# Attention scores of two branches: from full-height products, one head at a time, to 64-row products for two heads

## The chip, the cores and the metric

One core of a Trainium2 chip (trn2) runs the whole kernel. The metric is the device time of one execution in microseconds (us). Before the change it is 309.70 us, the median of three runs (309.48 to 309.84).

## The reference, cut to what matters

A decoder layer with two causal attention branches over the same input (512 tokens, width 1024), all in float32:

```
h = x @ w_in[l]
(qa, ka, va, ga, iq, ik, iw, c_q, c_kv, k_rope, gb) = _split_cols(h)
qa, ka = _rope(qa), _rope(ka)                  # 8 heads of 64
# branch A: each query attends to the 128 keys that a small indexer picked
att = einsum('bthd,btkhd->bhtk', qb, ks) * 64 ** -0.5 ; softmax ; @ v
# branch B: low-rank queries and keys; 64 plain and 32 rotated columns per head
s = (einsum('bthd,bshd->bhts', qn, k_nope) + einsum('bthr,bsr->bhts', qp, k_pe)) * 96 ** -0.5
# the rotated key k_pe is one for all 8 heads ; causal softmax ; @ v
out = concat([o_a * silu(ga), o_b * silu(gb)]) @ w_out[l]
x = layernorm(ALPHA * x + out)
```

## The kernel before

The products are wanted at nearly float32 accuracy. A number is split into a high part of type fp32r and the rest, a low part of type fp32r; TensorE (PE) takes three products, high by high, high by low and low by high. Where operands are left in plain f32, one product call is recorded as two matmuls.

**Stages.** (1) Seven groups of input projections, 8 chunks of 128 rows of `w_in` each, in three products per chunk and token tile (L1067, the helper `products`). ACT makes the high parts of the weights (L496), POOL the low parts (L403). (2) The latent projections for branch B: A_QPE (rotated query columns, 4 token tiles), A_QN (plain query columns, transposed, one PSUM bank for each pair of heads), later A_KN (plain key columns, the same way) and A_VB (values). (3) Branch A's attention, 32 units (L1216, L1219). (4) Branch B's attention, 32 units (L1225), with the output projection of finished token tiles laid in between (L1348, `out_products`). (5) The rest of the output projection and the layer norm.

**Units.** A unit u is one head of one tile of 128 queries. The tiles go in the order 3, 2, 1, 0, so that a unit's keys number N = 512, 384, 256, 128, eight units of each; `NU_A` = 32 units are branch A, the next 32 are branch B. For a unit, PE makes the scores in bank u % 2 of `ps_s`, DVE adds the mask and takes the row maximum (`mask_unit`, L887), ACT takes the exponential (`exp_unit`, L611), PE transposes it (L1275) two units later, ACT copies it (L631; in branch B, DVE adds the low part, `probs_low`, L927), and PE multiplies by the values four units later (L1291 in branch A, L1306 in branch B). The order on every engine is written out by hand: one loop over u on each, in which PE issues `scores(u)`, `transposes(u-2)`, `outputs(u-4)` and then what is due at this u (`PET_AT`, `O_FIRST`, `A_HALF_AT`). `scores(u)` waits until the mask of unit u-2 is done, `transposes` until a bank of `ps_pT` is free and the exponential is there.

**Branch A's scores.** `qaT` and `kaT` hold for every head the high part in 64 partitions and the low part in the other 64. One product of `qaT` with `kaT` gives high by high plus low by low; one with `kaT_swap`, the same array with its halves exchanged by eight DMAs (L329), gives the cross terms. So a unit costs two full-height fp32r products.

**Branch B's scores.** `qbT` and `kbT` hold 96 partitions for each head, 64 plain and 32 rotated, in plain f32: one product call a unit (L1225), two matmul records. ACT and DVE copy them out of PSUM in halves (L617, L895). The rotated query columns are transposed at u = `PET_AT` = 8 (L1242, 8 transposes), the rotated key at u = 14 (L1249, 4 transposes) and copied to all heads by a DMA (L347). Their values go to SBUF by four copies on ACT (L603), four on DVE (L872) and one on ACT (L685).

**Output weights.** SP loads eight pieces of `w_out` (k = 0 to 7): k < 4 into `w_raw`, the others into `wo_early`. POOL casts them to `wo_hi` (L444) and, for k < 4, makes the low part (L448), in the order `WO_ORDER`. `oT0`, into which ACT writes at u = `O_FIRST` + 2 = 24 (`copy_oT_hi(0, 0)`, L645), lies on `wo_early`, so that ACT waits there until all sixteen `wo_hi` halves are written.

Of the kernel before, what the change touches and what calls it, by code (L numbers as in the profile page):

```python
# [6 lines left out]
P = 128  # L7
# [20 lines left out]
def build(nc, x, xT, positions, freqs, w_in, q_norm_g, w_uq, kv_norm_g, w_ukv, w_out, ln_g, ln_b, out):  # L28
# [81 lines left out]
    qbT = sb("qbT", 0, [B_QK, B_HEADS, SEQ])  # L110
    kaT_swap = sb("kaT_swap", 178, [P, A_HEADS, SEQ], f32r)
# [6 lines left out]
    x_res = sb("x_res", 178, [P, 2, D_MODEL])  # L118
    lng = sb("lng", 186, [P, D_MODEL])
# [15 lines left out]
    kaT = sb("kaT", 98, [P, A_HEADS, SEQ], f32r)  # L135
# [4 lines left out]
    kbT = sb("kbT", 114, [B_QK, B_HEADS, SEQ])  # L140
# [8 lines left out]
    qaT = sb("qaT", 162, [P, A_HEADS, SEQ], f32r)  # L149
# [33 lines left out]
    iw, half_pi = col(TT * IDX_HEADS), col(1)  # L183
# [7 lines left out]
    with ExitStack() as ctx:  # L191
# [13 lines left out]
        kaT_swapped, kpe_copied, stored = sem("kaT_swapped"), sem("kpe_copied"), sem("stored")  # L205
# [51 lines left out]
        A_QPET, A_KPET = A_END + 2, A_END + 6  # L257
# [7 lines left out]
        ACC_LAST = [last_seen([*range(A_END), A_QPET, A_QPET + 1, A_KPET], b) for b in range(4)]  # L265
# [41 lines left out]
        def _(sp):  # L307
# [17 lines left out]
            for n in range(F_KT, F_END):  # L325
                sp.wait_ge(side_read[n % 4], seen(n) + 2)
                h = 2 * (n - F_KT)
                for a in range(2):
                    sp.dma_start(kaT_swap[A_DIM * a:A_DIM * (a + 1), h:h + 2, :].bitcast(f32),  # L329
                                 kaT[A_DIM * (1 - a):A_DIM * (2 - a), h:h + 2, :].bitcast(f32)).then_inc(kaT_swapped, 16)  # L330
# [6 lines left out]
            for k in range(1, KT // 2):  # L337
                load(C_OUT // 2 + k)
# [3 lines left out]
            sp.wait_ge(acc_ready, A_END + 2)  # L342
            load(C_OUT // 2)
            for k in (6, 7):
                load_early(k)
            sp.wait_ge(acc_read[2], ACC_LAST[2])
            sp.dma_start(kbT[NOPE:B_QK, 1:B_HEADS, :],  # L347
                         kbT[NOPE:B_QK, 0:1, :].broadcast_to([ROPE_D, B_HEADS - 1, SEQ])).then_inc(kpe_copied, 16)
            sp.wait_ge(scores_ready, NU_A)
            for k in range(KT // 2, KT):  # L350
                sp.dma_start(wo_raw_b[:, k - KT // 2], w_out_v[:, k]).then_inc(raw_b_loaded[k - KT // 2], 16)
            sp.dma_start(lng[:, :], ln_g.broadcast_to([P, D_MODEL])).then_inc(ln_loaded, 16)
# [15 lines left out]
        def _(pool):  # L368
# [10 lines left out]
                               base=0, pattern=[[-1, P]], channel_multiplier=1).then_inc(const_ready, 1)  # L379
            def rotate_queries(m):  # L380
# [30 lines left out]
            for m in range(TT):  # L411
# [13 lines left out]
                pool.tensor_tensor(src[:, :, 0], t1[:, :, 0], t2[:, :, 0], ALU.subtract).then_inc(qpe_rotated, 1)  # L425
                pool.tensor_tensor(src[:, :, 1], t1[:, :, 1], t2[:, :, 1], ALU.add).then_inc(qpe_rotated, 1)
# [55 lines left out]
        def _(act):  # L482
# [58 lines left out]
            def high_parts(first, i):  # L541

                dst, n = (qaT if first == F_QT else kaT), first + i
                act.wait_ge(side_ready, n + 1)
                for a in range(2):
                    rows = slice(A_DIM * a, A_DIM * (a + 1))
                    act.activation(dst[rows, 2 * i + a, :], side[rows, n % 4], ACT.Copy).then_inc(a_hi_ready, 1)
# [51 lines left out]
            def evac_qpeT(j):  # L599

                quad, r = divmod(j, 2)
                act.wait_ge(acc_ready, A_END + quad + 1)
                ins = act.activation(qbT[NOPE:B_QK, 4 * quad + r, :], ps_y[32 * r:32 * r + 32, quad], ACT.Copy)  # L603
                if r == 1:
                    ins.then_inc(acc_read[2 + quad], 1)

# [59 lines left out]
            for u in range(NU + T_LAG):  # L666
# [14 lines left out]
                if 0 <= u - PET_AT - 1 < 4:  # L681
                    evac_qpeT(u - PET_AT - 1)
                if u == PET_AT + 7:
                    act.wait_ge(acc_ready, A_END + 3)
                    act.activation(kbT[NOPE:B_QK, 0, :], ps_y[0:ROPE_D, 0], ACT.Copy).then_inc(acc_read[2], 2)  # L685
# [14 lines left out]
        def _(dve):  # L700
# [112 lines left out]
            dve.sem_inc(kpe_rotated, 1)  # L813
# [45 lines left out]
            for first, dst in ((F_QT, qaT), (F_KT, kaT)):  # L859
                for h in range(A_HEADS):  # L860
                    n, a = first + h // 2, h % 2
                    rows, low = slice(A_DIM * a, A_DIM * (a + 1)), slice(A_DIM * (1 - a), A_DIM * (2 - a))
                    dve.wait_ge(a_hi_ready, 2 * (n - F_QT) + a + 1)
                    ins = V.tensor_tensor(dst[low, h, :], side[rows, n % 4], dst[rows, h, :], ALU.subtract)
                    if a == 1:
                        ins.then_inc(side_read[n % 4], 2)

            def evac_qpeT(j):
# [131 lines left out]
            for u in range(NU):  # L1000
                if u >= 2:
                    mask_unit(u)
# [389 lines left out]
PET_AT = 8  # L1392
# [45 lines left out]
```

## Time and profile before

| | |
|---|---|
| median of 3 runs | 309.70 us |
| the profiled execution itself | 309.57 us |
| its span, first to last instruction | 307.7 us |
| mean granted TensorE clock | 0.995 |
| PE busy (matmuls) | 294.7 us, 96% of the span |
| PEld busy (weight loads) | 253.4 us, 82% |
| DVE, ACT, POOL busy | 235.3, 170.9, 158.7 us |
| stage 3, branch A's attention | about 177 to 214.5 us |
| stage 4, branch B's attention | about 214.5 to 278 us |

Busy time of an engine is the time in which at least one of its instructions runs. Matmuls overlap: the next one starts while the last one is still running out, so what a matmul costs in a dense stream is the distance from its start to the next start, not its own duration. The chain of waits gives that distance: it follows the work that ended last backwards and charges each piece only with the time until the next. A row of a table of stretches gives, after its length, the busy time of PE, PEld, DVE, ACT and POOL in that order. A row of a timeline begins with its start, then its length, the engine, the line, the operation, `out<-in`, the shape and how many instructions were merged; in brackets stands how long the engine sat idle before it and who released it.

### The profile page before, as it was taken

To read this page: it belongs to the slowest core of one execution; us is meant where nothing else is said; L and a number is where in the kernel's file an instruction comes from. 1 tells how busy PE (TensorE), PEld (TensorE's weight loads), DVE (VectorE), ACT (ScalarE), POOL (GpSimd) and SP (SyncE) were. 2 spreads that over 40 slices of the span, in tenths; PEclk is the share of its full clock that TensorE was granted. 3 is DMA by queue.
4 is the path that set the end of the run, shared out by engine and by line. 5 is a ranking of instruction groups with operands and counts; after the bars stand their busy time and mean duration, and the time that the engine had idled before them with its cause. 6 is when DMAs were issued, how large, how long until landed. Compare 5 with 4: busy or idle time off the path is not lost.

```text
span 307.7 us, 5163 instructions
## 1 busy us (share of the span) xinstructions
PE 294.7 (96%) x1646; PEld 253.4 (82%) x1646; DVE 235.3 (76%) x540; ACT 170.9 (56%) x411; POOL 158.7 (52%) x180
## 2 busy tenths in 40 slices
PE   7979999999999999999999999999999999999990
PEld 7969988888888888888889789998677777888890
DVE  1959967888999999996043644855789998987785
ACT  5843274575242262374357787998867885554200
POOL 4869855303999975535326697820492010335211
PEclk9999999999999999999999999999999999999998
DMA  7947442200434532320058333230950000040411
GB/s 253 342 129 207 136 139 71 68 2 0 117 91 136 154 112 78 102 68 2 0 136 205 140 137 117 90 62 8 350 192 0 2 0 3 0 137 2 136 68 68
DMA packets 14777, 31.24 MB, mean 102 GB/s; under 512 B 1728, under 2 KB 4288, under 8 KB 14752
## 3 DMA queue, kind: packets, MB, share of 16 engines
q1 hardware_dynamic: 14192, 30.60, 32.6%
q10 hardware_dynamic: 560, 0.33, 0.4%
q8 instruction: 13, 0.21, 0.3%
q14 instruction: 12, 0.10, 0.1%
HBM read 26.28 MB, written 2.10 MB: 92 GB/s over the span
## 4 chain that ended last, share of the span: by engine, by line
PE 87%; DVE 5%; issue 2%; DMA 2%; ACT 2%; SPq 0%; POOL 0%; DVEq 0%; ACTq 0%; POOLq 0%
PE ps L1067 46%; PE ps L1348 14%; PE ps L1275 6%; PE ps L1225 5%; PE ps L1291 5%; PE ps L1306 3%; PE ps L1216 2%; DMA w_raw<-in_w_in 2%; PE ps L1219 2%; PE ps L1132 1%; DVE x_lo L717 1%; PE ps L1151 1%; PE ps L1320 1%; PE ps L1122 1%; ACT oT L645 1%
## 5 line engine op out<-in xcount | busy, mean ns | idle before, releaser
L403 POOL TENSOR_TENSOR w_lo<-w_raw,w_hi 128x512 fp32r<-128x512 f32 (+3 forms) x62 | 79.3, 1298 | 41.1 <-ACT w_hi L496 41.0
L1067 PE MATMUL ps<-w_hi,x_hi 128*128 128x512 f32 (+2 forms) x220 | 83.2, 378 | 2.9 <-POOL w_lo L403 1.5
L1067 PE MATMUL ps<-w_hi,x_lo 128*128 128x512 f32 (+2 forms) x220 | 82.0, 373 | 0.0
L1067 PE MATMUL ps<-w_lo,x_hi 128*128 128x512 f32 (+2 forms) x220 | 82.0, 373 | 0.0
L496 ACT ACTIVATE w_hi<-w_raw 128x512 fp32r<-128x512 f32 (+3 forms) x62 | 36.2, 591 | 73.3 <-PE ps L1067 72.3
L1067 PEld LDWEIGHTS ps<-w_hi,x_hi 128*128 128x128 f32 x220 | 41.4, 188 | 9.8 <-issue 2.7
L1067 PEld LDWEIGHTS ps<-w_hi,x_lo 128*128 128x128 f32 x220 | 41.3, 188 | 6.5
L1067 PEld LDWEIGHTS ps<-w_lo,x_hi 128*128 128x128 f32 x220 | 41.4, 188 | 5.9
L1348 PE MATMUL ps<-wo_hi,oT 128*128 128x512 f32 (+1 forms) x144 | 44.3, 372 | 0.0
L611 ACT ACTIVATE probs<-probs,small 128x512 f32<-128x512 f32 (+3 forms) x64 | 35.7, 558 | 11.0 <-DVE small L887 10.5
L1275 PE MATMUL ps<-ident,probs 128*128 128x128 f32 x160 | 28.3, 274 | 1.9 <-ACT probs L611 0.9
L1275 PEld LDWEIGHTS ps<-ident,probs 128*128 128x128 f32 x160 | 20.1, 140 | 11.3 <-issue 6.3
L1348 PEld LDWEIGHTS ps<-wo_hi,oT 128*128 128x128 f32 x144 | 25.7, 189 | 3.3
L840 DVE MATCH_REPLACE8 score<-small,score 128x256 f32<-128x256 f32 (+2 forms) x48 | 25.6, 542 | 0.0
L887 DVE CUSTOM_DVE_ANT_0 probs<-ps,score 128x512 f32<-128x512 f32 (+2 forms) x24 | 13.3, 556 | 14.4 <-PE ps L1219 14.4
L837 DVE MAX8 small<-score 128x8 f32<-128x256 f32 (+2 forms) x48 | 23.5, 545 | 0.0
L1225 PE MATMUL ps<-kbT,qbT 96*128 96x512 f32 (+3 forms) x64 | 22.7, 435 | 0.0
L1291 PE MATMUL ps<-va,probsT 128*128 128x64 f32 x160 | 21.4, 264 | 0.0
L1291 PEld LDWEIGHTS ps<-va,probsT 128*128 128x128 f32 x160 | 20.6, 193 | 0.6 <-issue 0.6
L295 POOL TENSOR_TENSOR obT<-half_sum,crossed 64x128 f32<-64x128 f32 x16 | 8.3, 516 | 24.7 <-DVE oT L919 13.7
L887 DVE CUSTOM_DVE_ANT_0 probs<-ps,causal 128x128 f32<-128x128 f32 (+3 forms) x40 | 17.6, 444 | 3.6 <-PE ps L1225 1.6
L631 ACT ACTIVATE probsT_b<-ps 128x512 fp32r<-128x512 f32 (+3 forms) x32 | 13.8, 431 | 8.4 <-PE ps L1275 8.2
(170 smaller groups left out, 557.4 us busy)
## 6 DMA issues: line engine op xcount, KB each, us to landing
w_raw<-in_w_in SPq DMA_DIRECT2D x20, 512.0 KB, 3.6
kaT_swap<-kaT SPq DMA_DIRECT2D x8, 256.0 KB, 3.7
w_raw<-in_w_out SPq DMA_DIRECT2D x4, 512.0 KB, 5.8
wo_early<-in_w_out SPq DMA_DIRECT2D x4, 512.0 KB, 4.2
wo_raw_b<-in_w_out SPq DMA_DIRECT2D x4, 512.0 KB, 5.1
x_res<-in_x SPq DMA_DIRECT2D x4, 512.0 KB, 7.1
w_raw<-in_w_in SPq DMA_DIRECT2D x4, 416.0 KB, 3.7
x_raw<-in_xT SPq DMA_DIRECT2D x3, 512.0 KB, 6.4
```

The costliest lines, as they stand in the source:

```text
L403: pool.tensor_tensor(w_lo[:, s, 0:n], w_raw[:, s, 0:n], w_hi[:, s, 0:n], ALU.subtract).then_inc(w_lo_ready, 1)
L496: act.activation(dst, w_raw[:, s, 0:n], ACT.Copy).then_inc(w_hi_ready, 1)
L611: act.activation(probs[:, u % NPROBS, 0:N], probs[:, u % NPROBS, 0:N], ACT.Exp, bias=neg_max[:, u % 8:u % 8 + 1], scale=-1.0, accum_out=ro ...
L631: act.activation(dst, ps_pT[:, slot_of[u] % 2, 0:N], ACT.Copy).then_inc(probsT_copied, 1)
L837: step(V.max(top8[:, 8 * j:8 * j + 8], sc))
L840: step(V.match_replace(out=sc, in_to_replace=top8[:, 8 * j:8 * j + 8], in_values=sc, imm_value=TAKEN))
L887: V.tensor_tensor_reduce(out=probs[:, u % NPROBS, 0:N], in0=ps_s[:, u % 2, 0:N], in1=bias, scale=-scale, scalar=3.0e38, op0=ALU.add, op1=A ...
L1067: ins = mm(dst, a, b, start=start and j == 0, stop=stop and j == len(pairs) - 1)
L1225: ins = mm(ps_s[:, b, 0:N], qbT[:, h, t], kbT[:, h, 0:N], start=True, stop=True)
L1275: ins = nc.tensor.transpose(bank[:, j * P:(j + 1) * P], probs[:, u % NPROBS, j * P:(j + 1) * P], ident[:, :])
L1291: ins = mm(ps_o[:, v % 2, h * A_DIM:(h + 1) * A_DIM], probsT[:, u % 3, j * P:(j + 1) * P], va[:, j, h * A_DIM:(h + 1) * A_DIM], start=(j = ...
L1348: ins = mm(out_ps(i, b), oT[i % 2][:, o, k, :], w[:, wcols], start=(r == 0), stop=(r == 3 * KT - 1))
```

## The change

Both branches compute the scores of the two heads of a pair together. The two heads of a pair lie in the two halves of the partitions: head 2p in partitions 0 to 63, head 2p+1 in 64 to 127. High and low parts are separate arrays (`qa_hi`, `qa_lo`, `ka_hi`, `ka_lo`, `qn_hi`, `qn_lo`, `kn_hi`, `kn_lo`). For each term, PE issues one product over 64 rows for the first head and one for the second, into the two banks of `ps_s`. Branch A has three terms, so six products a pair in place of four; branch B has three for the plain columns and two for the rotated ones, so ten fp32r products a pair in place of two f32 product calls (four matmul records).

The rotated query of a head is stored twice in 64 rows (`qr`): its high part in 32 rows and its low part in the next 32; the rotated key's high part (`kr_hi`) and low part (`kr_lo`) are repeated in all four groups of 32 rows. The duplicates are made before the transposes: POOL writes `qpe_dup`, DVE writes `kpe_dup`; then five banks of four transposes each, one bank at each entry of `ROPE_AT`, ACT's high copy and DVE's scalar_tensor_tensor or subtract for each.

Scores, masks and the wait between them go in pairs: PE issues both units of a pair at even u after all earlier masks, DVE masks both at even u. The DMAs that exchanged halves and copied the rotated key are gone. `qpe_dup` lies on a part of `w_raw`, so the loads of the output weights k = 0, 2, 3 move behind the fourth bank of rotated transposes and `WO_ORDER` changes. The loads of the layer norm's constants and of x move behind the last product of branch A with its values.

```
-            for k in range(1, KT // 2):
-                load(C_OUT // 2 + k)
+            load(C_OUT // 2 + 1)
             sp.wait_ge(acc_ready, A_END)
             for k in (4, 5):
                 load_early(k)
-            sp.wait_ge(acc_ready, A_END + 2)
-            load(C_OUT // 2)
             for k in (6, 7):
                 load_early(k)
-            sp.wait_ge(acc_read[2], ACC_LAST[2])
-            sp.dma_start(kbT[NOPE:B_QK, 1:B_HEADS, :],
-                         kbT[NOPE:B_QK, 0:1, :].broadcast_to([ROPE_D, B_HEADS - 1, SEQ])).then_inc(kpe_copied, 16)
+            sp.wait_ge(acc_ready, A_END + 4)
+            for k in (0, 2, 3):
+                load(C_OUT // 2 + k)
...
-                for a in range(2):
-                    rows = slice(A_DIM * a, A_DIM * (a + 1))
-                    act.activation(dst[rows, 2 * i + a, :], side[rows, n % 4], ACT.Copy).then_inc(a_hi_ready, 1)
+                act.activation(dst[:, i, :], side[:, n % 4], ACT.Copy).then_inc(a_hi_ready, 1)
...
+            def rope_high(i):
+
+                act.wait_ge(acc_ready, A_END + i + 1)
+                dst = qr[:, i, :] if i < B_HEADS // 2 else kr_hi[:, :]
+                act.activation(dst, ps_y[:, i % 2], ACT.Copy).then_inc(b_hi_ready, 1)
...
-            for first, dst in ((A_QN, qbT), (A_KN, kbT)):
+            for first, dst in ((A_QN, qn_hi), (A_KN, kn_hi)):
                 for p in range(4):
                     act.wait_ge(acc_ready, first + p + 1)
-                    act.activation(dst[0:NOPE, 2 * p, :], acc[0:NOPE, p], ACT.Copy).then_inc(acc_read[p], 1)
+                    act.activation(dst[:, p, :], acc[:, p], ACT.Copy).then_inc(b_hi_ready, 1)
...
+            def rope_low(i):
+
+                dve.wait_ge(b_hi_ready, 8 + i + 1)
+                if i < B_HEADS // 2:
+                    dve.wait_ge(low_rows_ready, 4)
+                    ins = V.scalar_tensor_tensor(out=qr[:, i, :], in0=qr[:, i, :], scalar=low_rows, in1=ps_y[:, i % 2],
+                                                 op0=ALU.mult, op1=ALU.add)
+                else:
+                    ins = V.tensor_tensor(kr_lo[:, :], ps_y[:, i % 2], kr_hi[:, :], ALU.subtract)
+                ins.then_inc(acc_read[2 + i % 2], 2)
...
-            for first, dst in ((A_QN, qbT), (A_KN, kbT)):
+            for first, hi, lo in ((A_QN, qn_hi, qn_lo), (A_KN, kn_hi, kn_lo)):
                 for p in range(4):
-                    dve.wait_ge(acc_ready, first + p + 1)
-                    V.tensor_copy(dst[0:NOPE, 2 * p + 1, :], acc[NOPE:P, p]).then_inc(acc_read[p], 1)
+                    dve.wait_ge(b_hi_ready, (4 if first == A_KN else 0) + p + 1)
+                    V.tensor_tensor(lo[:, p, :], acc[:, p], hi[:, p, :], ALU.subtract).then_inc(acc_read[p], 2)
...
-                if u >= 2:
+                if u >= 2 and u % 2 == 0:
                     mask_unit(u)
+                    mask_unit(u + 1)
...
             def scores(u):
+
                 v, m, h, N = unit(u)
...
+                else:
+                    pe.wait_ge(masked_ready, u)
...
-                    mm(ps_s[:, b, 0:N], qaT[:, h, t], kaT[:, h, 0:N], start=True, stop=False)
-                    if u == 0:
-                        pe.wait_ge(kaT_swapped, 16 * A_HEADS)
-                    ins = mm(ps_s[:, b, 0:N], qaT[:, h, t], kaT_swap[:, h, 0:N], start=False, stop=True)
+                    terms = [(q[:, p], k[:, p]) for q, k in ((qa_hi, ka_hi), (qa_hi, ka_lo), (qa_lo, ka_hi))]
                 else:
-                    ins = mm(ps_s[:, b, 0:N], qbT[:, h, t], kbT[:, h, 0:N], start=True, stop=True)
-                ins.then_inc(scores_ready, 1)
+                    terms = [(q[:, p], k[:, p]) for q, k in ((qn_hi, kn_hi), (qn_hi, kn_lo), (qn_lo, kn_hi))]
+                    terms += [(qr[:, p], kr_hi), (qr[:, p], kr_lo)]
+                for j, (q, k) in enumerate(terms):
+                    for a in range(2):
+                        rows = slice(A_DIM * a, A_DIM * (a + 1))
+                        ins = mm(ps_s[:, a, 0:N], q[rows, t], k[rows, 0:N], start=j == 0, stop=j == len(terms) - 1)
+                        if j == len(terms) - 1:
+                            ins.then_inc(scores_ready, 1)
...
             for u in range(NU + PV_LAG):
-                if 2 <= u < NU:
+                if 2 <= u < NU and u % 2 == 0:
                     scores(u)
...
-                if u == PET_AT:
-                    qpe_transposes()
-                if u == PET_AT + 6:
-                    kpe_transposes()
+                if u + 1 in ROPE_AT:
+                    rope_transposes(ROPE_AT.index(u + 1))
...
-PET_AT = 8
-WO_ORDER = (1, 2, 3, 4, 5, 6, 7, 0)
+ROPE_AT = [9, 10, 12, 13, 15]
+WO_ORDER = (1, 4, 5, 6, 7, 0, 2, 3)
```

## Rows read from the trace of the kernel before

**Rows 1.** The page's chain of work that ended last, by engine
```profile
PE 87%; DVE 5%; issue 2%; DMA 2%; ACT 2%; SPq 0%; POOL 0%; DVEq 0%; ACTq 0%; POOLq 0%
```
**Rows 2.** Stretches: start:end, length, busy (instructions) by engine, clock, DMA share, GB/s
```profile
207.00:215.00 8.00, 7.38 (x62) 6.82 (x61) 4.47 (x22) 6.56 (x29) 0.70 (x1) 1.00 0.00 0
215.00:230.00 15.00, 15.00 (x79) 10.40 (x78) 11.84 (x28) 11.26 (x29) 10.16 (x8) 1.00 0.83 282
230.00:244.50 14.50, 14.50 (x87) 11.40 (x86) 13.79 (x36) 11.51 (x32) 2.60 (x3) 1.00 0.00 1
```
**Rows 3.** Timeline of PE in branch A, at N = 512, then 384, then 256
```profile
180.57 0.48 PE L1216 MATMUL ps<-kaT,qaT 128*128 128x512 f32 x1
180.89 0.39 PE L1219 MATMUL ps<-kaT_swap,qaT 128*128 128x512 f32 x1
181.12 0.60 PE L1275 MATMUL ps<-ident,probs 128*128 128x128 f32 x4
...
193.31 0.42 PE L1216 MATMUL ps<-kaT,qaT 128*128 128x384 f32 x1
193.74 0.49 PE L1275 MATMUL ps<-ident,probs 128*128 128x128 f32 x3
...
205.62 0.36 PE L1216 MATMUL ps<-kaT,qaT 128*128 128x256 f32 x1
205.95 0.38 PE L1275 MATMUL ps<-ident,probs 128*128 128x128 f32 x2
```
**Rows 4.** Chain of waits (start, us, what), branch B, one unit each at N = 512, 384, 256, 128
```profile
225.65 0.86 PE ps L1225 x2
...
234.17 0.65 PE ps L1225 x2
...
250.66 0.43 PE ps L1225 x2
...
266.03 0.22 PE ps L1225 x2
```
**Rows 5.** Chain of waits, from branch A's first scores on
```profile
171.26 5.67 PE ps L1067 x24
...
182.56 0.28 PE ps L1216
...
187.83 0.88 PE ps L1242 x8
```
**Rows 6.** Timelines of ACT, then DVE, over the start of branch A
```profile
170.39 0.59 ACT L617 ACTIVATE qbT<-ps 64x512 f32<-64x512 f32 x1 [0.77 <-PE ps L1067]
171.85 0.73 ACT L611 ACTIVATE probs<-probs,small 128x512 f32<-128x512 f32 x1 [0.87 <-DVE small L887]
...
173.28 2.02 ACT L617 ACTIVATE kbT<-ps 64x512 f32<-64x512 f32 x4
...
171.73 0.68 DVE L887 CUSTOM_DVE_ANT_0 probs<-ps,score 128x512 f32<-128x512 f32 x1
...
172.45 2.52 DVE L895 COPY kbT<-ps 64x512 f32<-64x512 f32 x4
```
**Rows 7.** Timeline of PE: transposes that use 32 columns (`128*32`), then its next load
```profile
197.38 0.60 PE L1249 MATMUL ps<-ident,kpe_tok 128*32 128x128 f32 x4
197.71 0.19 PEld L1216 LDWEIGHTS ps<-kaT,qaT 128*128 128x128 f32 x1
```
**Rows 8.** Timelines of SP's queue, POOL and ACT: output weights and their first user
```profile
189.40 1.45 SPq L335 DMA_DIRECT2D wo_early<-in_w_out  x2
...
180.77 1.17 POOL L444 CAST wo_hi<-w_raw 128x512 fp32r<-128x512 f32 x2
182.02 2.52 POOL L448 TENSOR_TENSOR wo_lo_a<-w_raw,wo_hi 128x512 fp32r<-128x512 f32 x2
...
193.64 2.42 POOL L444 CAST wo_hi<-wo_early 128x512 fp32r<-128x512 f32 x4 [3.14 <-DMA wo_early<-in_w_out]
...
209.06 0.60 ACT L645 ACTIVATE oT<-ps 128x512 fp32r<-128x512 f32 x1 [0.49 <-PE ps L1320]
```

More of the change, by code:

```diff
@@ L263, in last_seen @@
             return seen([n for n in fills if n % 4 == bank][-1]) + 2
-        ACC_LAST = [last_seen([*range(A_END), A_QPET, A_QPET + 1, A_KPET], b) for b in range(4)]
+        ACC_LAST = [last_seen([*range(A_END), *A_QPET, A_KPET], b) for b in range(4)]
         SIDE_LAST = [last_seen(range(F_END), b) for b in range(4)]
@@ L379, in _ @@
                                base=0, pattern=[[-1, P]], channel_multiplier=1).then_inc(const_ready, 1)
+            pool.wait_ge(const_ready, 5)
+            for r in range(4):
+                pool.memset(low_rows[ROPE_D * r:ROPE_D * (r + 1)], -float(r % 2)).then_inc(low_rows_ready, 1)
+                pool.wait_ge(low_rows_ready, r + 1)
             def rotate_queries(m):
@@ L424, in _ @@
                 pool.wait_ge(q_step, 4 * (TT + m + 1))
-                pool.tensor_tensor(src[:, :, 0], t1[:, :, 0], t2[:, :, 0], ALU.subtract).then_inc(qpe_rotated, 1)
-                pool.tensor_tensor(src[:, :, 1], t1[:, :, 1], t2[:, :, 1], ALU.add).then_inc(qpe_rotated, 1)
+                for a, op in enumerate((ALU.subtract, ALU.add)):
+                    both = [t[:, :, a].unsqueeze(2).broadcast_to([P, B_HEADS, 2, FREQ_B]) for t in (t1, t2)]
+                    pool.tensor_tensor(qpe_dup[:, m, :, :, FREQ_B * a:FREQ_B * (a + 1)], both[0], both[1],
+                                       op).then_inc(qpe_rotated, 1)
             def scale_gate(i):
@@ L541, in high_parts @@
             def high_parts(first, i):
-                dst, n = (qaT if first == F_QT else kaT), first + i
+                dst, n = (qa_hi if first == F_QT else ka_hi), first + i
                 act.wait_ge(side_ready, n + 1)
-                for a in range(2):
-                    rows = slice(A_DIM * a, A_DIM * (a + 1))
-                    act.activation(dst[rows, 2 * i + a, :], side[rows, n % 4], ACT.Copy).then_inc(a_hi_ready, 1)
+                act.activation(dst[:, i, :], side[:, n % 4], ACT.Copy).then_inc(a_hi_ready, 1)
             for g in range(NG):
@@ L680, in _ @@
                     exp_unit(u)
[L681 to L685, printed above, removed]
+                if u in ROPE_AT:
+                    rope_high(ROPE_AT.index(u))
                 if u == VB_EARLY:
@@ L856, in _ @@
                 dve.sem_inc(k_rotated, 1)
[L859 to L868, printed above, removed]
-                quad, r = divmod(j, 2)
-                dve.wait_ge(acc_ready, A_END + quad + 1)
-                ins = V.tensor_copy(qbT[NOPE:B_QK, 4 * quad + 2 + r, :], ps_y[64 + 32 * r:96 + 32 * r, quad])
-                if r == 1:
-                    ins.then_inc(acc_read[2 + quad], 1)
+            for first, hi, lo in ((F_QT, qa_hi, qa_lo), (F_KT, ka_hi, ka_lo)):
+                for i in range(A_HEADS // 2):
+                    n = first + i
+                    dve.wait_ge(a_hi_ready, n - F_QT + 1)
+                    V.tensor_tensor(lo[:, i, :], side[:, n % 4], hi[:, i, :], ALU.subtract).then_inc(side_read[n % 4], 2)
+            def rope_low(i):
[7 more added lines that the diff above has]
+                ins.then_inc(acc_read[2 + i % 2], 2)
             def mask_unit(u):
@@ L1226, in scores @@
-                ins.then_inc(scores_ready, 1)
-            for u in range(2):
-                scores(u)
+                if u == 0:
+                    for b in range(2):
+                        pe.wait_ge(side_read[b], SIDE_LAST[b])
+                    for n in range(F_QT, F_END):
+                        pe.wait_ge(side_read[n % 4], seen(n) + 2)
+                else:
+                    pe.wait_ge(masked_ready, u)
+                if u == NU_A:
+                    for p in range(4):
+                        pe.wait_ge(acc_read[p], ACC_LAST[p])
@@ L1230, in _ @@
+            scores(0)
             wait_chunk(C_UKV)
```

84 lines of the change are left out of this document (37 added, 47 removed).

## The prediction

> **What bounds the kernel now.** I read the chain of waits first. PE carries 87% of it, no other engine more than 5% [rows 1], so PE's stream is the path and I price the change by the distance from one matmul's start to the next. Second, the table of stretches, to see who is next behind PE. In branch A's last stage (N = 128) PE is not full, 7.38 of 8.00 us, and in branch B from 230 to 244.5 DVE is busy 13.79 of 14.50 us beside a full PE: there PE can gain 0.7 us at most before DVE is the bound. From 215 to 230 DVE has room, 11.84 of 15.00 [rows 2]. Third, the timelines, for the prices of one unit.
>
> **Prices.** In branch A at N = 512 the first product starts at 180.57, the second at 180.89, the transposes at 181.12: 0.55 us a unit, of which 0.23 is each product's pitch and 0.09 an entry cost, a weight load that the short matmuls ahead don't hide. At N = 384 it is 0.43 (193.31 to 193.74, pitch 0.17), at N = 256 0.33 (205.62 to 205.95, pitch 0.12) [rows 3]. Branch B's f32 unit costs 0.86, 0.65, 0.43 and 0.22 us [rows 4], 3.6 to 3.8 times the fp32r pitches down to N = 256. The eight transposes of 128 columns took 0.88 us [rows 5], so a load and a short matmul have a floor of 0.11 us a record; I take that as the pitch at N = 128.
>
> **The open price: two products in the two row halves.** No matmul of the kernel before uses less than 96 rows. The bounds: two such products cost one pitch (they run beside each other), or two. Between them lies a third value: the matmuls run beside each other but each still needs its 0.11 us of load or dispatch, 0.22 for two. I take one pitch, with the loads also side by side, because the two products share neither rows nor a PSUM bank and alternate strictly. That is a choice; the trace doesn't decide it.
>
> Beside this choice stands the Trainium skill, "TensorE: Matmul & The Clock Gate", section "Part 3: Packing small matmuls": products in different row groups run concurrently, and four of 32 rows were measured 3.07 times faster than one after the other. It was not measured there on fp32r streams with a new load each. By the page the sum is the forecast below; no row here shows it.
>
> **Branch A's scores, per pair.** N = 512: before 2 x 0.55 = 1.10, after 3 x 0.23 + 0.09 = 0.78; three of the four pairs are counted in the start, below, one runs steadily: -0.3. N = 384: 0.86 to 3 x 0.17 + 0.09 = 0.60, four pairs: -1.0. N = 256: 0.66 to 3 x 0.12 + 0.09 = 0.45, four pairs -0.8, of which I take -0.6, since ACT comes close behind PE there. N = 128: from about 0.52 to 0.42 at best, on a stretch that PE does not fill; both masks must now end before the next pair's scores, which is as long; 0. Sum -1.9.
>
> **Branch B's scores, per pair, five terms.** N = 512: 1.72 to 5 x 0.23 = 1.15, four pairs: -2.3. N = 384: 1.30 to 0.85, four pairs would be -1.8; DVE allows 0.7: -0.7. N = 256: 0.86 to 0.60, four pairs -1.0, half taken because DVE remains as full: -0.5. N = 128: 0.44 to 5 x 0.11 = 0.55, four pairs: +0.4. Sum -3.1.
>
> **The start of branch A.** Before, the 24 products behind the first scores ran without a gap from 171.26 to 176.93 [rows 5], since ACT and DVE each emptied half a bank. Now DVE's low part waits for ACT's whole copy. Scores of pair 0: 170.35 to 171.03. DVE: last low part of the queries from 170.98 (ACT's copy begins at 170.39) to 171.6, two masks to 172.9 at 0.62 each. ACT: two exponentials at 0.71 until 173.8, then four copies at 0.50: 174.3, 174.8, 175.3, 175.8; DVE's subtractions at 0.62 end at 174.9, 175.5, 176.1, 176.8 [rows 6]. PE finishes the key products at 173.75 and needs these banks one by one for the value products (0.68 each): it ends at 177.7, 0.75 late. By unit 6 (before: 182.56), with the second pair's wait for two masks against 0.6 saved on scores, I get 0.6 late: +0.6. What is queued behind the waiting value product is all of PE's loop. Bounds: 0 (the idle time at 179.2 swallows it) and +1.2.
>
> **Transposes and copies of the rotated parts.** 20 transposes in place of 12 at 0.11: +0.9 on PE, with nothing to hide it. ACT has five large copies before and after, DVE four copies against five; at 0.6 to 0.7 us each, the one more lies in DVE's idle time of branch A. The doubled writes of POOL end well before u = 8; the earlier halving of ACT's and DVE's work on q and k lies beside projections: 0 both. Removing eight half-swapping DMAs and the key's copy: 0, no row has PE waiting for them; bound 0 to -0.2.
>
> **Output weights moved behind u = 12.** Before, a k < 4 costs POOL 3.7 us (0.6 a cast, 1.25 a subtraction) and a load lands 4.2 us after its issue (189.40 to 193.64) [rows 8]. Now k = 0, 2, 3 are issued when the fourth bank is transposed, near 195; the first lands at 199.5 to 201, POOL adds 3.7 + 3.7 + 1.2, so the sixteenth `wo_hi` is there at 208.1 to 209.6. ACT reaches its wait at u = 24 near 208.5 (its copy ran at 209.06, released by PE, not POOL [rows 8]). Queued behind it are the exponentials of N = 128, and PE's transposes wait for these: 0 to +1.1, I take +0.4. The products of u = 34 near 218 need the low parts, done by 212: 0. The later loads of the layer norm's constants are needed near 257: 0.
>
> **Changes between full-height and half-height products.** 32 pairs, in and out: 64 changes. Nearest row: before and after transposes that use 32 columns PE's records keep their 0.11 pitch, the next load starts at 197.71 with no gap [rows 7]; that limits columns, not rows, so 0 is only the low bound, and I take it. The high bound is a full run-out, 0.39 - 0.23 = 0.16 [rows 3], or with a load that can't be hidden 0.27; times 64 that is 10 to 17 us.
>
> The rule against the change stands in the Trainium skill, "TensorEngine Tiling (Array Packing)", section "Tiling Modes": changing the tiling mode drains TensorE. No row here shows a change of row mode; the third rival prices it.
>
> **Sum.** -1.9 - 3.1 + 0.6 + 0.9 + 0.4 = -3.1 us on the profiled execution's 309.57, hence 306.5; that execution lies 0.13 under the median, so 306.6. Its own range: without DVE's limits, the wait for the output weights and half the start -5.5 (304), with the start, that wait and a little entry cost at their upper ends -0.7 (309).
>
> **Rivals.**
> First, the floor of 0.11 a record stays, so that a term of a pair costs at least 0.22. For: every load in branch A's short stretches is at that pitch. Against: the halves share no rows. Branch A: -0.3, then (0.70 against 0.86) -0.6, (0.70 against 0.66) +0.2, and half of +0.7, +0.4, in the last stage. Branch B: -2.3, (1.10 against 1.30) -0.8, (1.10 against 0.86) +1.0, (1.10 against 0.44) +2.6, sum +0.5. With +0.6, +0.9, +0.4 the whole is +2.1: 311.8. It is slower, and it decides from N below 512 on.
> Second, the halves run one after the other. Branch A: start +1.3, then +0.4, +1.0, +0.6, +0.4; rotated +0.9; branch B: four pairs each of 2.30 against 1.72, 1.70 against 1.30, 1.20 against 0.86, 1.10 against 0.44: +7.9. Sum +12.5: 322. Against: nothing but the disjoint rows and banks.
> Third, the halves run together but each change of mode makes PE run out. At 0.11 a change 64 cost 7.0: -3.1 + 7.0 = +3.9, 313.6. It outweighs the gain from 0.05 us a change on. The place to see it is the first half-height product after a matmul and the first transpose after the scores.
> Fourth, the halves run together, but the scores of a pair wait for two masks, and DVE, 95% busy from 230 to 244.5 [rows 2], sets the pace of branch B from N = 384 on. Then branch A keeps -1.0 of its -1.9 and branch B -0.9 of its -3.1, which the costs of +1.9 cancel: 309.6. For: DVE's share; against: at N = 512, where most of the gain is, DVE has a fifth of its time left.
>
> **How the numbers follow.** Forecast 46%, first rival 20%, second 9%, third 16%, fourth 9%. No change means within 0.2%, 0.6 us, about what this measurement can tell. Faster: the forecast, a quarter of the fourth and a little of the third below its break-even: 0.50. Same: the fourth's rest and the edges of the first and the forecast: 0.11. Slower 0.39. The likeliest case's own range is 304 to 309; the range over the cases reaches down to 303.5 and up to 314.5, which takes in the first rival and most of the third and leaves out the second.
>
> **What would show it.** In the timeline after, the two products of a term at N = 512: starts nearly together and 0.23 from term to term (forecast), 0.11 apart with 0.23 or 0.22 for the two (first rival, seen at N = 128), 0.23 apart (second). An entry of over 0.1 us before and after each pair: third. PE's pitches for all scores add up to some 30 us before (eight units of each N: 0.55, 0.43, 0.33, 0.26 in branch A, 0.86, 0.65, 0.43, 0.22 in branch B) and should be near 22 after (four pairs of each N, eight terms in both branches at 0.23, 0.17, 0.12, 0.11, and 16 entries of 0.09). PE idle for some 0.8 us among the value products near 175: the start. ACT's copy at u = 24 released by POOL: the output weights. The forecast is wrong if the pair at N = 512 in branch B takes over 1.4 us, or if DVE is less than 95% busy from there to N = 256 while PE idles.

## The result: 8.4 us slower

The changed kernel takes 318.16 us (median of four runs, 317.72 to 318.65) against 309.77: ratio 1.027, 95% interval 1.0258 to 1.0282. The forecast was 306.6, the range 303.5 to 314.5. The profiled execution is one of the two at the top of these four, 318.65 us, span 316.8, mean granted clock 0.986; the two at 317.7 and 317.8 had 0.992 and 0.995. The profiled one has a stretch at half clock, described in the last section, and the mean clock of the other upper one, 0.987, points to the same. So the median holds about 0.4 us of it: against an experiment without that stretch the changed kernel counts as 317.75, and each difference to 318.16 below is then 0.4 smaller for an experiment that is faster, and 0.4 larger for one that is slower.

The chain of waits by engine, for the changed kernel: PE's share falls from 87% [rows 1] to 79%, DVE and ACT rise.

```profile
PE 79%; DVE 8%; issue 4%; ACT 4%; DMA 2%; DVEq 0%; SPq 0%; POOL 0%; ACTq 0%; POOLq 0%
```

**Do the halves run beside each other?** Yes. The timeline of PE, one pair at N = 512 in branch B of the changed kernel; each row merges the two products of a term (`64*128`, x2):

```profile
230.99 0.40 PE L1351 MATMUL ps<-wo_lo_a,oT 128*128 128x512 f32 x1
231.31 0.50 PE L1227 MATMUL ps<-kn_hi,qn_hi 64*128 64x512 f32 x2
231.65 0.40 PE L1227 MATMUL ps<-kn_lo,qn_hi 64*128 64x512 f32 x2
231.88 0.41 PE L1227 MATMUL ps<-kn_hi,qn_lo 64*128 64x512 f32 x2
232.11 0.41 PE L1227 MATMUL ps<-kr_hi,qr 64*128 64x512 f32 x2
232.35 0.41 PE L1227 MATMUL ps<-kr_lo,qr 64*128 64x512 f32 x2
232.69 0.66 PE L1278 MATMUL ps<-ident,probs 128*128 128x128 f32 x4
233.10 0.72 PE L1309 MATMUL ps<-probsT_b,vb_parts 128*128 128x256 f32 x4
```

From term to term it is 0.23 us for two products, as forecast. But the first half-height product starts 0.32 after the full-height one ahead of it (0.23 would do), the second term 0.34 after the first, the first transpose 0.34 after the last term, and the next work 0.41 after that, where it was 0.35 without a change of height. Four delays, 0.09, 0.11, 0.11 and 0.06: 0.37 us a pair, 0.18 for each change. The chain, here of the pair before it, shows the same sum: 1.38 for the ten products (1.15 forecast) and 0.59 for the four transposes behind them (0.44 elsewhere).

```profile
227.10 1.38 PE ps L1227 x10
228.48 0.59 PE ps L1278 x4
229.06 0.47 PE ps L1309 x4
229.54 0.46 PE ps L1351 x2
230.00 0.44 PE ps L1278 x4
```

So a pair at N = 512 in branch B costs 1.38 + 0.15 = 1.53 against 1.72 before (two of 0.86 [rows 4]), not 1.15. It is still the cheaper one, but at N = 256 the same sum is 0.79 + 0.15 = 0.94 against 0.86. The delays do not shrink with N: at N = 384 they are 0.09, 0.11, 0.09 and 0.07. In branch A, against the full-height terms of experiment 1 in the same place, they are about 0.12, 0.02, 0.10 and 0.05, 0.29 a pair: there full-height products have most of the second delay too, behind the value products.

**Stages.** Start of the first score product of each stage, read from the timelines of PE; the last column is the start of the last eight transposes of the gates, from where PE's stream is the same in both:

```
                    A 512   A 384   A 256   A 128   B 512   B 384   B 256   B 128   tail
before              170.2   186.0   199.1   207.5   214.6   230.0   244.5   261.7   285.6
changed             170.5   188.1   202.5   211.9   219.4   235.6   251.0   268.6   294.1
late by               0.3     2.1     3.4     4.4     4.8     5.6     6.4     6.9     8.4
full-height terms   170.4   187.3   200.6   209.8   217.1   231.3   247.6   264.6   288.8
products put back   170.4   187.5   201.3   210.6   217.9   233.6   248.8   266.3   290.2
  and start mended  170.4   185.9   199.7   209.1   216.3   232.1   247.3   264.8   288.7
only pairs, before  170.5   186.2   199.2   207.8   215.0   230.8   246.0   263.5   287.4
```

The loss builds up everywhere; it is not one wait. The last column says 8.4 us for the profiled execution with its stretch at half clock; this execution is 9.1 us over the one of the kernel before, and the other 0.7 lies behind the last stores. Before, the execution ends 5.3 us after SP issued them (at 304.30), now 6.0 us after (at 312.69). In the changed kernel's trace one packet that the profile gives as of kind "instruction", on queue q14, runs among the packets of these stores, and nine of their packets come in singly behind the rest, over a last 1 us. The same end, 5.9 to 6.1 us with such a packet, is in every experiment built on the changed kernel except the two of experiment 11; those end after 5.4 us, and the kernel before and experiments on it after 5.2 to 5.3, without it. That the one packet holds back the nine is not tested.

At the very start PE sits idle, in the timelines of PE, ACT and DVE of the changed kernel:

```profile
174.07 0.39 PE L1069 MATMUL ps<-latT_hi,w_lo 128*128 128x512 f32 x1
175.53 0.50 PE L1069 MATMUL ps<-w_hi,latT_hi 128*128 128x512 f32 x1 [1.08 <-DVE kn_lo L896]
```
```profile
172.68 0.72 ACT L616 ACTIVATE probs<-probs,small 128x512 f32<-128x512 f32 x1 [1.44 <-DVE small L888]
173.41 0.71 ACT L616 ACTIVATE probs<-probs,small 128x512 f32<-128x512 f32 x1
174.11 2.04 ACT L622 ACTIVATE kn_hi<-ps 128x512 fp32r<-128x512 f32 x4
```
```profile
171.96 0.68 DVE L888 CUSTOM_DVE_ANT_0 probs<-ps,score 128x512 f32<-128x512 f32 x1
174.79 2.48 DVE L896 TENSOR_TENSOR kn_lo<-ps,kn_hi 128x512 fp32r<-128x512 f32 x4 [1.53 <-ACT kn_hi L622]
```

The value products need banks that DVE empties only after ACT's copies, which stand behind two exponentials [compare rows 6].

### The profile page after: what moved, and what is told of

It is laid out like the page before. It is cut to its first block, busy times and chain, and to the rows that moved or that the text cites. A ratio compares the mean times of both kernels' runs of the same rounds, so it can differ in the third digit from the quotient of the medians.

```text
span 316.8 us, 5428 instructions
## 1 busy us (share of the span) xinstructions
PE 299.6 (95%) x1782; PEld 253.1 (80%) x1782; DVE 230.3 (73%) x534; ACT 166.0 (52%) x403; POOL 161.0 (51%) x184
## 4 chain that ended last, share of the span: by engine, by line
PE 79%; DVE 8%; issue 4%; ACT 4%; DMA 2%; DVEq 0%; SPq 0%; POOL 0%; ACTq 0%; POOLq 0%
PE ps L1069 44%; PE ps L1351 13%; PE ps L1227 7%; PE ps L1278 5%; PE ps L1294 3%; DVE probs L888 2%; PE ps L1309 2%; DMA w_raw<-in_w_in 2%; DVE x_lo L719 1%; PE ps L1134 1%; ACT probs L616 1%; PE ps L1153 1%; PE ps L1124 1%; PE ps L1323 1%; DVE probsT_b L928 1%
## 5 line engine op out<-in xcount | busy, mean ns | idle before, releaser
L1278 PE MATMUL ps<-ident,probs 128*128 128x128 f32 x160 | 30.0, 287 | 2.6 <-DVE probsT_b L928 1.6
L1278 PEld LDWEIGHTS ps<-ident,probs 128*128 128x128 f32 x160 | 18.7, 145 | 11.7 <-issue 4.8
L888 DVE CUSTOM_DVE_ANT_0 probs<-ps,causal 128x128 f32<-128x128 f32 (+3 forms) x40 | 16.4, 447 | 5.9 <-PE ps L1227 5.6
L636 ACT ACTIVATE probsT_b<-ps 128x512 fp32r<-128x512 f32 (+3 forms) x32 | 13.8, 430 | 12.4 <-PE ps L1278 12.2
L888 DVE CUSTOM_DVE_ANT_0 probs<-ps,score 128x512 f32<-128x512 f32 (+2 forms) x24 | 12.4, 553 | 10.6 <-PE ps L1227 10.6
L636 ACT ACTIVATE probsT<-ps 128x512 f32<-128x512 f32 (+3 forms) x32 | 13.8, 431 | 8.7 <-PE ps L1278 8.6
```

The source lines that it names most:

```text
L636: act.activation(dst, ps_pT[:, slot_of[u] % 2, 0:N], ACT.Copy).then_inc(probsT_copied, 1)
L888: V.tensor_tensor_reduce(out=probs[:, u % NPROBS, 0:N], in0=ps_s[:, u % 2, 0:N], in1=bias, scale=-scale, scalar=3.0e38, op0=ALU.add, op1=A ...
L1278: ins = nc.tensor.transpose(bank[:, j * P:(j + 1) * P], probs[:, u % NPROBS, j * P:(j + 1) * P], ident[:, :])
```

## Experiments

All times are medians; 309.7 to 309.9 us is the kernel before beside them. Where heads are mixed or parts left out, the run tells of time only. Only the profiled execution of experiments 3 and 10 (its first kernel) has a stretch at half clock.

**1. Full-height terms.** In `scores`, one product over all rows for each term, alternating between the banks; in short:

```
-    for a in range(2):
-        rows = slice(A_DIM * a, A_DIM * (a + 1))
-        ins = mm(ps_s[:, a, 0:N], q[rows, t], k[rows, 0:N], ...)
+    ins = mm(ps_s[:, j % 2, 0:N], q[:, t], k[:, 0:N], ...)
```

> The changed kernel with each term of a pair's scores as one product over all 128 rows (three in branch A, five in branch B, alternating between the two banks) in place of two over 64 rows side by side. The scores mix the two heads; everything else, the number of pitches, the pairs, the masks, the waits, is as in the changed kernel. Theory 1 (each change between full-height and half-height products costs about 0.18 us, from 1.52 us for a pair at N = 512 in branch B where five pitches are 1.15; 64 changes, 11.5 us on PE): 308 to 311 us, the rest hidden by DVE and ACT. Theory 2 (the order costs it: masks in pairs, the copy waits at the start and for the rotated parts): 316 to 318 us.

313.52 us, ratio 1.0121 (1.0106 to 1.0136). Changes of height cost 4.6 us in all (4.2 without the half clock), under half of the 10.5 us that 16 x 0.37 + 16 x 0.29 would be on PE. The time lies between the two theories, in the range of neither. Where the rest of PE's free time went shows the table of stretches of this run; the pairs behind the length are PE, PEld, DVE, ACT, POOL:

```profile
217.10:231.30 14.20, 13.36 (x83) 11.49 (x84) 11.39 (x26) 11.08 (x30) 8.57 (x7) 1.00 0.74 284
231.30:247.60 16.30, 13.94 (x92) 11.76 (x91) 15.34 (x40) 11.48 (x33) 4.28 (x4) 1.00 0.02 9
```

At N = 384 of branch B, PE is idle for 2.4 of 16.3 us while DVE is busy for 15.3, and the stage is longer than before (14.6). The stage ahead of it was 1.2 us shorter, so DVE has more to do here; both together take 30.5 us against 30.0, with DVE busy for 26.7 against 25.6. In the table of waits over the whole run (us in total, times, longest) the first two rows of PE's weight loads are:

```profile
PEld ps L1232 <- DVE small L888: 4.4, 6, 1.0
PEld ps L1282 <- DVE probsT_b L928: 3.2, 2, 1.7
```

**2. One term at half height.** The same, except that the second term stays as two half-height products (the condition `j != 1` for a full-height term).

> As the changed kernel, but only the first term... here: every term over all 128 rows except the second one, which stays as two products over 64 rows. The scores mix heads. Two changes of height before and two after that term's neighbours: one in, one out, as often as in the changed kernel (64 in all). Theory 1: the same as the changed kernel, 317 to 319 us. If the cost belongs to each half-height product and not to the change: a third to a fifth of it is left, 310 to 312 us. Theory 2: 316 to 318 us.

319.48 us, ratio 1.0332 (1.0301 to 1.0364): as slow as with all terms at half height, even a little slower, and 0.5 over theory 1's range. What costs is the change, not the half-height product. In its timeline, a pair in branch B, N = 512:

```profile
231.81 0.40 PE L1232 MATMUL ps<-kn_hi,qn_hi 128*128 128x512 f32 x1
232.14 0.49 PE L1232 MATMUL ps<-kn_lo,qn_hi 64*128 64x512 f32 x2
232.56 0.50 PE L1232 MATMUL ps<-kn_hi,qn_lo 128*128 128x512 f32 x1
232.91 0.40 PE L1232 MATMUL ps<-kr_hi,qr 128*128 128x512 f32 x1
233.15 0.39 PE L1232 MATMUL ps<-kr_lo,qr 128*128 128x512 f32 x1
```

Starts are 0.33, 0.42, 0.35, 0.24 apart, where 0.23 is the pitch.

**3. A change at every term.** Half height for even terms, full height for odd ones (`j % 2 == 1`).

> As the changed kernel, with the odd terms over all 128 rows and the even terms as two products over 64 rows, so that the height changes at every term: 4 changes a pair in branch A, 6 in branch B, 160 in place of 64. The scores mix heads. Theory 1: 96 more changes at 0.18 us are 17 us, 331 to 336 us. Theory 2: 317 to 320 us.

336.86 us, ratio 1.088 (1.0861 to 1.09), 18.7 us over the changed kernel for 96 more changes. The number is not clean: the granted clock was 0.50 from 224 to 236 and 0.59 until 238, with PE busy almost all along, which by an estimate (half of 12 us) is 6 of the 18.7. At full clock a pair at N = 512 took 2.17 us in the chain for five terms, and the transposes behind it 0.15 more than elsewhere. With 1.15 for the five terms, 1.17 us are left for six changes, 0.20 each:

```profile
242.26 2.17 PE ps L1232 x8
244.42 0.59 PE ps L1282 x4
```

**4. One head after the other.** The two loops exchanged, `for a in range(2)` outside.

> The changed kernel with the products of a pair in another order: all terms of the first head, then all of the second. Nothing else is changed, the scores are the same. If two half-height products run beside each other only when they alternate between the row halves, each now costs its own pitch: 3 x 4 x 0.63 more in branch A and 5 x 4 x 0.63 in branch B (0.23, 0.17, 0.12, 0.11 at the four N), 20 us: 334 to 339 us. If they never ran beside each other: 318 us. Both theories expect the first; the rival of the prediction (one after the other) the second.

320.23 us, ratio 1.0336 (1.032 to 1.0351): only 2.1 us more (2.5 without the half clock), not 20. Both expectations missed, and the timeline says why. The program has all five terms of the first head before those of the second; PE started them interleaved:

```profile
230.34 0.50 PE L1227 MATMUL ps<-kn_hi,qn_hi 64*128 64x512 f32 x1
230.68 0.40 PE L1227 MATMUL ps<-kn_lo,qn_hi 64*128 64x512 f32 x1
230.69 0.49 PE L1227 MATMUL ps<-kn_hi,qn_hi 64*128 64x512 f32 x1
230.92 0.39 PE L1227 MATMUL ps<-kn_hi,qn_lo 64*128 64x512 f32 x1
231.02 0.39 PE L1227 MATMUL ps<-kn_lo,qn_hi 64*128 64x512 f32 x1
```

The second head's first product starts 0.35 after the first head's, beside its second term; the pair takes 1.70 in place of 1.38, where ten pitches in a row would be 2.3.

**5. Masks one at a time again.** DVE masks unit u at u (`if u >= 2: mask_unit(u)`).

> The changed kernel with DVE masking one unit at each u, as in the kernel before, in place of two at each even u; PE still issues both units' scores together. With full-height terms in the same places the kernel took 313.5 us, so 4.6 of the 8.4 us belong to the changes of height and 3.8 to something else. Theory A (masks in pairs hold back DVE's low parts, and PE waits for those from N = 384 of branch B on): 315 to 316.5 us. Theory B (the rest is the start and the eight more transposes, the order of the masks is harmless): 317.5 to 318.5 us.

323.03 us, ratio 1.0442 (1.0407 to 1.0476): 4.9 us slower, far over both theories. Theory A falls in this form. Once both units' scores go in one call, the next call waits for both masks, and a mask taken one u later holds up PE: its weight loads for the scores wait 13.8 us for DVE's masks, in 18 waits, where it was 2.0 us in 4. The same edit on the kernel of experiment 1 has the same sign:

> Full-height terms (three and five a pair, heads mixed in the scores) and one mask at each u. 313.5 us with masks in pairs. Theory A: 311 to 312 us, what is left being the start (+1) and the transposes (+0.9) against fewer pitches. Theory B: 313 to 314 us.

319.14 us, ratio 1.0306 (1.0283 to 1.0328), 5.6 over 313.5.

**6. The start.** ACT's first exponentials moved behind its copies of the keys' banks:

```
             for first, dst in ((A_QN, qn_hi), (A_KN, kn_hi)):
                 ...
-                if first == A_QN:
-                    for u in range(2):
-                        exp_unit(u)
+            for u in range(2):
+                exp_unit(u)
```

> The changed kernel with ACT's first two exponentials behind its copies of the keys' banks in place of ahead of them, so that PE's value products find their banks. In the changed kernel PE sat idle some 1.4 us there (174.3 to 175.5, and the products behind). If that wait is on the path: 316.7 to 317.2 us. If the first transposes, which need these exponentials, or a later wait take it back: 318 us.

316.08 us, ratio 1.0202 (1.0185 to 1.0219), 2.1 less, or 1.7 without the half clock. That wait was on the path.

**7. Pairs alone, in the kernel before.** `scores(u); scores(u + 1)` and both masks at even u, waiting for all earlier masks.

> The kernel before with its own score products, but in pairs: at even u PE issues the scores of u and u+1 when all earlier masks are done, and DVE masks both. No half-height products, no change in copies or transposes. Theory A (pairs cost by themselves): 311.5 to 313 us. Theory B (they are harmless): 309.5 to 310.3 us.

311.13 us, ratio 1.0044 (1.0029 to 1.0059). Pairs cost 1.4 us by themselves, 0.4 under theory A's range. By the table above, the loss comes in branch B, from N = 512 to N = 256.

**8. One branch's products put back.** In the changed kernel, branch B's scores as one f32 product over 96 rows a head:

```
+    mm(ps_s[:, a, 0:N], qn_hi[0:B_QK, p, t].bitcast(f32), kn_hi[0:B_QK, p, 0:N].bitcast(f32), ...)
```

> The changed kernel with branch B's scores as one plain f32 product over 96 rows for each head (two matmul records, as in the kernel before) in place of ten products over 64 rows a pair; branch A stays as changed, pairs and copies too. The low parts and the rotated parts are left out of branch B's scores (time only). If a pair costs what the changed trace shows (1.52, 1.22, 0.93, 0.85 us at the four N, the two changes of height in it, against 1.72, 1.30, 0.86, 0.44): four pairs each, 0.9 us faster, 316.5 to 317.7 us. If changes of height were free, as forecast: 3 us slower, 321 us.

316.32 us, ratio 1.0209 (1.0193 to 1.0225), 1.8 less (1.4 without the half clock). Then branch A's as two full-height products a head, with branch B as changed:

> The changed kernel with branch A's scores as two full-height fp32r products a head, four a pair, as many as before the change; branch B stays as changed. The scores of branch A mix heads (time only). The changed trace gives 1.05, 0.87, 0.70, 0.60 us a pair against 1.10, 0.86, 0.66, 0.52: 0 to 0.5 us faster, 317.5 to 318.3 us. If changes of height were free: 2 us slower, 320 us.

316.03 us, ratio 1.0197 (1.0179 to 1.0216), 2.1 less (1.7 without the half clock, which alone makes 1.0 of the difference between the two profiled executions, from 219 to 235). The prices a pair that were expected missed two things: the changed pair's first product starts 0.12 later behind the value products, and four full-height products in a row have one entry, 0.78 us at N = 384 and not 0.86. Undoing either half of the change makes the kernel faster.

**9. All products put back.** Both edits together:

> The changed kernel with the score products of both branches as before the change in number, height and type (four full-height fp32r products a pair in branch A, one f32 product over 96 rows a head in branch B), all else as changed: pairs, copies, start, transposes, loads. Scores mix heads or leave parts out (time only). If the parts add: undoing branch A's gave 2.1 us, branch B's 1.8, so 314.2 us, and the surroundings alone cost 4.4 us (start 2.1, pairs 1.4, transposes 0.9). If the two overlap in what they free (the half clock near 219): 315 us.

314.88 us, ratio 1.0168 (1.0153 to 1.0183). The score products cost 3.3 us net (2.9 without the half clock); everything around them 5.2 us. With the start mended:

> The same with the first two exponentials behind the keys' copies. If the start costs 1.5 to 2.1 us here as well: 312.1 to 312.8 us. What is left over before is the pairs (1.4) and the transposes (0.9).

313.28 us, ratio 1.0114 (1.0099 to 1.0129), 1.6 less. With 12 transposes of rotated parts in place of 20:

> The same again with two in place of four transposes in each of the four banks of rotated queries, 12 in all as before the change; half of the rotated queries is left out (time only). Eight at 0.11 us: 0.9 us less, 311.2 to 311.9 us. If they lie beside ACT's and DVE's copies: no change.

312.71 us, ratio 1.0096 (1.0079 to 1.0113), 0.6 less, two thirds of 0.9.

**10. Low parts of the rotated banks one u later.** `if u - 1 in ROPE_AT: rope_low(...)`, first on the kernel of experiment 6, then on 313.28:

> The changed kernel, correct scores, with the first two exponentials behind the keys' copies (316.1 us) and DVE's low parts of the rotated banks one u later, so that ACT's high copy is there when DVE comes to them. If DVE's wait for ACT ahead of the masks is on the path: 315.0 to 315.5 us. If it lies beside PE's work: 316.1 us; if the later low parts hold up the next bank's transposes: 316.5 us and more.

316.36 us, ratio 1.0203 (1.0182 to 1.0225), runs from 315.5 to 316.9. Its profiled execution has the stretch at half clock (0.50 from 218 to 221) and that of experiment 6 hasn't. Its two executions at a mean clock of 0.994 and 0.996 took 315.5 and 315.9, 0.2 to 0.6 under experiment 6: the direction of a gain, too few to tell its size.

> The same edit where the score products are put back and the start is mended (313.3 us): 312.3 to 312.7 us if the wait is on the path, 313.3 us if not.

312.52 us, ratio 1.0089 (1.0074 to 1.0104), 0.8 less: DVE's wait for ACT ahead of the masks was on the path.

**11. Four merges moved to POOL.** `POOL_PAIRS = 4`, which takes 0.6 us a pair off DVE from pair 4 to pair 7, and POOL's `scale_gate(1)` behind the merge of pair 6.

> Full-height terms (no change of height, heads mixed), the first two exponentials behind the keys' copies, and the merges of pairs 4 to 7 of branch B on POOL in place of DVE (2 x 0.3 us a pair off DVE). From 313.5 us the start takes 2.1: 311.4. Theory (DVE, 15.34 of 16.30 us busy from N = 384 of branch B on while PE idles 2.4 us, takes the gain): the merges give another 1.5 to 2.4, 309.0 to 310.0 us. Rival (PE's idle time there is latency of the pairs, not DVE's load): 311 to 311.5 us.

310.58 us, ratio 1.0021 (1.0011 to 1.003), 2.9 less than experiment 1. The start takes 1.6 of it (experiment 9), and 0.6 lies behind the last stores, where the late packet is gone; so the merges give about 0.7, under half of what the theory wanted. They could not do what it asked: POOL's first moved merge starts at 247.7, and the stage N = 384, which ends at 246.0, takes 16.3 us as in experiment 1. In it DVE is still busy for 14.0 of 15.0 us and PE idle for 1.6, so whether DVE's load or the order of the pairs sets that stage stays open:

```profile
229.50:244.50 15.00, 13.36 (x86) 11.14 (x84) 14.04 (x36) 11.02 (x31) 4.48 (x4) 1.00 0.05 19
```

> The changed kernel, correct scores, with the first two exponentials behind the keys' copies (316.1 us) and the merges of pairs 4 to 7 on POOL. PE idles 0.9 us of that stage in the changed kernel: 315.0 to 315.8 us; if DVE's load isn't the bound there: 316.1 us.

315.09 us, ratio 1.0169 (1.0152 to 1.0185), 1.0 less than experiment 6, 0.4 of it behind the last stores. And in the kernel before:

> The kernel before with the merges of pairs 4 to 7 of branch B on POOL in place of DVE, all else as before. Before, PE has no idle time from 230 to 244.5 although DVE is 95% busy: 309.4 to 309.9 us, no change. If DVE's load showed already: 308.8 to 309.3 us.

309.01 us (ten runs, 308.65 to 309.22), ratio 0.9976 (0.9967 to 0.9985). This is the one version that beats both kernels, by 0.24%: DVE showed already, in the stage that these merges belong to. Until the first N = 256 unit of branch B it is no earlier (244.8 against 244.5), the first moved merge starting at 246.85; that stage then takes 16.5 us in place of 17.2, in its table of stretches:

```profile
244.50:261.00 16.50, 15.82 (x96) 13.46 (x95) 13.50 (x39) 12.20 (x37) 4.69 (x9) 1.00 0.00 0
```

## Why the prediction was wrong, step by step

The runs split the 8.4 us into three steps, one kernel to the next: surroundings +5.2 (products put back over before), pitches saved -1.4 (full-height terms under products put back), changes of height +4.6 (changed over full-height terms, with 0.4 of half clock in it). They add up to +8.4 because the steps follow one another; in another order each could have another size. The forecast had +1.9, -5.0 and 0. Its own sign of being wrong is there: a pair at N = 512 in branch B takes 1.53 us, over its limit of 1.4.

- **The open price** (two halves, one pitch): right, at every N. At N = 128 the chain has 0.70 us for ten products with their entry, so not even the floor of 0.11 a record holds for two in different halves. The first and second rivals are refuted. (The first rival's sum was a little off: three terms of 0.22 with an entry of 0.09 are 0.75, not 0.70, at N = 384 and 256 of branch A, which makes it some 312.3.)
- **Changes between heights** (taken as 0): the first step that failed, and wrongly chosen among its bounds. The nearest row [rows 7] was of limited columns and says nothing of rows. A change took 0.18 us, in experiment 3 0.20, near the 0.16 of a run-out. The page that the prediction set against it, the Trainium skill's "TensorEngine Tiling (Array Packing)", section "Tiling Modes", says that changing the mode drains TensorE; the trace agrees, with this delay. The third rival had the right mechanism at 0.11 a change; at 0.18 its own formula, -3.1 + 64 x 0.18, gives +8.4, which is the measured number by accident, since only 4.6 of its 11.5 came through and the rest was made up elsewhere.
- **Branch A's and B's scores** (-1.9 and -3.1): the pitches did go, the time did not. Full-height terms (experiment 1) saved 1.4 us of the 5.0 against the products put back (experiment 9). What is saved on PE at N = 384 in branch B meets DVE at 94%, as forecast, but PE then loses ground, which I had bounded by 0. The scores of a pair wait for both masks and the masks stand behind DVE's low parts, sums and merges. That is the fourth rival's mechanism; the waits of experiment 1, the 1.4 us of experiment 7 and the 0.6 to 0.7 us that four merges give back from N = 256 on speak for it. How much of the stage N = 384 is DVE's load and how much the order of the pairs, no run separates.
- **The start** (+0.6): the mechanism and its place were right, the size was off: 1.6 (experiment 9) to 1.7 (experiment 6 without the half clock). DVE's first low part of the keys ended at 175.5, not 174.9, because the two masks began at 171.96, not 171.6; after that wait PE had nothing that caught up with it.
- **Rotated parts** (+0.9): PE's part measured 0.6. What I put at nothing, the one more DVE copy, was the error: it is not the 0.7 us of work but its place, DVE waiting for ACT's copy in front of the next masks, 0.8 with the products put back.
- **Output weights** (+0.4): 0. POOL's last cast ended at 211.4, and ACT's copy at 213.74 was released by PE.
- Of the 5.2 us around the products, 1.6, 0.6, 1.4 and 0.8 are accounted for (the 1.4 in another kernel). Of the 0.8 left, 0.7 lies behind the last stores, with the late packets, which the prediction had no term for; it is not shown what in the change brings them. Neither the halved copies of q and k nor the later loads were tried by themselves.

## What to carry to other kernels

Row halves do run two products in the time of one, but a kernel pays for every change between full and half height, here 0.15 to 0.20 us. On PE a visit to half height has to save more than 0.3 to 0.4 us: here five terms at N = 512 did (1.53 against 1.72), at N = 256 they did not. Before saving time on the bound engine, ask which engine is within a few per cent of it and in what order that one serves the other; a pair that must be masked as a pair takes away the slack of one unit. Work of no great length that is put in front of the next unit's masks costs its wait, even where its engine has idle time.

## What the runs showed of the hardware

- **Half-height products overtake.** In experiment 4 products started in another order than the program's: the second head's first product started at 230.69, ahead of three products of the first head that stand before it in the program. The Trainium skill, "TensorE: Matmul & The Clock Gate", section "Part 3: Packing small matmuls", says that matmuls start and end in program order; here the trace differs, and the pair's 1.70 us in place of 2.3 bears it out.
- **A stretch at half clock.** In the changed kernel's profiled execution the granted clock is 0.52, near the 1.2 GHz level, from 219.4 to 222, and ten products take 2.48 us in place of 1.38:

```profile
219.40:222.00 2.60, 2.58 (x11) 1.66 (x12) 0.11 (x1) 0.82 (x5) 0.00 (x0) 0.52 0.91 342
```

Ahead of it, from 211.9 to 219.4, PE was busy for 6.64 of 7.50 us with short products and gaps. In experiments 1 and 6 PE was busy for 6.13 of 7.30 and 6.66 of 7.50 us there and the clock stayed at 1.00, so it is not settled what brings it. It costs about 1 us: the changed kernel's own four runs differ by it (317.7 and 317.8 against 318.6), and so does the first kernel of experiment 10.

- **The end of an execution can move by 0.7 us behind the last instruction of every compute engine.** See the last stores above: the same stores, with 5.3 us or 6.0 us from their issue to the end.
